# Two feed-forwards of a hybrid decoder layer: gate and up by Strassen's seven half products, down as a phase of its own

## The chip, the cores and the metric

The kernel runs on 1 core of one Trainium2 chip. The metric is the device time of one execution in microseconds (us). All outputs are float32, and every large product is made in three passes over float32r halves: each operand is split into a rounded part (`hi`) and its rest (`lo`), and hi x hi, hi x lo and lo x hi are added up.

## The reference, cut to what matters

One layer for 1088 tokens (1024 of a prompt, 64 samples), of width 1024. The change touches the feed-forward at its start and the one at its end; the attention and state-space parts between them stay.

```python
D_MODEL = 1024
D_FF = 2816
def rmsnorm(x, g):
    xf = x.astype(jnp.float32)
    xf = xf * lax.rsqrt(jnp.mean(xf * xf, axis=-1, keepdims=True) + EPS)
    return (xf * g.astype(jnp.float32)).astype(x.dtype)

def swiglu_ffn(x, g, w_in, w_out):
    h = rmsnorm(x, g) @ w_in
    gate, up = jnp.split(h, 2, axis=-1)
    return (jax.nn.silu(gate) * up) @ w_out
...
    x = x + 0.5 * swiglu_ffn(x, lw['norm_ffn1'], lw['w_ffn1_in'], lw['w_ffn1_out'])
...
    x = x + 0.5 * swiglu_ffn(x, lw['norm_ffn2'], lw['w_ffn2_in'], lw['w_ffn2_out'])
```

## The kernel before, in words

x lies in SBUF transposed: 8 tiles of 128 features by 1092 token columns, in 3 groups of 364. `ffn_stage` runs twice, as `ffn1` and `ffn2`. D_FF is 22 tiles of 128 features; a chunk is two of them, so there are 11 chunks (a loop `Fori` over the middle ones).

**Normalization** (`FusedNorm`): ACT squares x and TensorE sums the squares (in `ffn2` the sums were made by the stage before, `summed_before`), ACT takes the root, DVE the reciprocal (L220), DVE scales (L234), ACT rounds (`h_hi`, L180), DVE makes the rest (`h_lo`, L212). **Gate and up** (`up`): for each feature tile and group, gate and then up, 8 k tiles of three matmuls each (`passes`, L307 to L309), into two pairs of PSUM banks `gu`. ACT takes Silu (L411); DVE multiplies (L518), rounds (L521) and makes the rest (L523). **Down** (`down`): for 8 output tiles x 3 groups, two feature tiles of three matmuls into one of four `dn` banks; DVE adds half of it to x (L532). It stands between the two gate-and-up halves of the next chunk. **Weights** come by DMA from SP's queue, 1 MB each (`load_up`, `load_down`), each into a single raw buffer; ACT rounds (L402, L421) and DVE makes the rest (L506, L543). GpSimd does nothing in a feed-forward. The order on each engine is written out by hand in `chunk`; semaphores join them. The last chunk (`close`) also squares the finished x tiles and sums them (L264) for the next normalization; in `ffn2` the final norm and the stores of y follow.

Of the kernel before, what the change touches and what calls it, by code (L numbers as in the profile page):

```python
# [15 lines left out]
P = 128  # L16
# [295 lines left out]
def ffn_stage(core, xT, gain, h_hi, h_lo, w_in, w_out, tag, gu_banks, dn, first_loads=None, arrivals=None,  # L312
# [3 lines left out]

    nc = core.nc
    chunks = FT // 2
    with ExitStack() as ctx:
        sb = lambda name, shape, dt=F32: ctx.enter_context(nc.sbuf_tensor(f"{tag}_{name}", shape, dt))  # L320
        up_raw = sb("up_raw", [P, 2 * KT * P])
        up_hi = sb("up_hi", [P, 2, 2, KT, P], F32R)
        up_lo = sb("up_lo", [P, 2, 2, KT, P], F32R)
        down_raw = sb("down_raw", [P, 2, D_MODEL])
        down_hi = sb("down_hi", [P, 2, D_MODEL], F32R)
        down_lo = sb("down_lo", [P, 2, D_MODEL], F32R)
        act_hi = sb("act_hi", [P, 3, TP], F32R)
        act_lo = sb("act_lo", [P, 3, TP], F32R)
        silu = sb("silu", [P, 2, TG])
        prod = sb("prod", [P, 2, TG])  # L330
        gu = gu_banks[:].rearrange("p (b u) c -> p b u c", u=2)
        up_landed, up_hi_ready, up_lo_ready = map(
            core.sem, ("up_landed", "up_hi_ready", "up_lo_ready"))
        down_landed, down_hi_ready, down_lo_ready = map(
            core.sem, ("down_landed", "down_hi_ready", "down_lo_ready"))
        gu_ready, silu_ready, prod_ready, act_hi_ready, act_ready = map(
            core.sem, ("gu_ready", "silu_ready", "prod_ready", "act_hi_ready", "act_ready"))
        dn_ready, dn_added = map(core.sem, ("dn_ready", "dn_added"))
        norm = FusedNorm(core, ctx, xT, gain, ((0, KT, core.mean_model),), h_hi, h_lo, f"{tag}_norm",
                         lambda u: dn[:, u, :], (silu, prod), arrivals, gain_landed, summed_before)  # L340
        running = RunningSquares(core, lambda g: gu_banks[:, g, :], core.mean_model,
                                 [silu[:, 0, :], silu[:, 1, :], prod[:, 0, :], prod[:, 1, :]])
        lag = 3
        closing = [(t, g) for g in range(GROUPS) for t in range(KT)]
        closed = (chunks - 1) * KT * GROUPS
        fin = None
        if final is not None:
            fin = FinalNorm(core, xT, final[0], running, norm.rms[:, 0, :], norm.inv[:, 0, :], final[1])

        def slot(par, f):  # L350
            return 2 if f else par

        def schedule(eng, chunk, last):

            chunk(0, 0, True, False)
            chunk(1, 1, True, True)
            chunk(2, 0, True, True)
            with eng.Fori(1, (chunks - 3) // 2) as it:
                chunk(it * 2 + 1, 1, True, True)
                chunk(it * 2 + 2, 0, True, True)  # L360
            chunk(chunks - 2, (chunks - 2) % 2, True, True)
            chunk(chunks - 1, (chunks - 1) % 2, False, True)
            last()

        with nc.Block() as block:

            @block.sync
            def _(sp):
                def load_up(n, guard):
                    if guard:  # L370
                        sp.wait_ge(up_lo_ready, n)
                    sp.dma_start(up_raw[:], w_in[bass.ds(n, 1)].rearrange("o p c -> (o p) c")
                                 ).then_inc(up_landed, 16)

                def load_down(c, guard):
                    if guard:
                        sp.wait_ge(down_lo_ready, c)
                    sp.dma_start(down_raw[:], w_out[bass.ds(c, 1)].rearrange("o p f c -> (o p) f c")
                                 ).then_inc(down_landed, 16)

                def chunk(c, par, more, full):
                    load_down(c, full)
                    if more:
                        load_up(c * 2 + 2, True)
                        load_up(c * 2 + 3, True)

                if first_loads is not None:
                    first_loads(sp, lambda: load_up(0, False))
                else:
                    load_up(0, False)  # L390
                load_up(1, True)
                schedule(sp, chunk, lambda: None)
                if fin is not None:
                    fin.stores(sp)

            @block.scalar
            def _(act):
                def split_up(n, s, reused):
                    act.wait_ge(up_landed, n * 16 + 16)
                    if reused:  # L400
                        act.wait_ge(gu_ready, (n - 1) * GROUPS)
                    act.activation(up_hi[:, s].rearrange("p u k c -> p (u k c)"), up_raw[:],  # L402
                                   ACT.Copy).then_inc(up_hi_ready, 1)

                def gate(c, f):
                    for g in range(GROUPS):
                        j = c * 6 + (3 * f + g)
                        act.wait_ge(gu_ready, j + 1)
                        if not (isinstance(c, int) and j < 2):
                            act.wait_ge(prod_ready, j - 1)  # L410
                        act.activation(silu[:, (f + g) % 2, :], gu[:, (f + g) % 2, 0, :TG],  # L411
                                       ACT.Silu).then_inc(silu_ready, 1)

                def chunk(c, par, more, full):
                    gate(c, 0)
                    if more:
                        split_up(c * 2 + 2, 0, True)
                    act.wait_ge(down_landed, c * 16 + 16)
                    if full:
                        act.wait_ge(dn_ready, c * (KT * GROUPS))  # L420
                    act.activation(down_hi[:].rearrange("p f c -> p (f c)"),  # L421
                                   down_raw[:].rearrange("p f c -> p (f c)"), ACT.Copy
                                   ).then_inc(down_hi_ready, 1)
                    gate(c, 1)
                    if more:
                        split_up(c * 2 + 3, 1, True)

                def close():
                    for d, (t, g) in enumerate(closing):
                        act.wait_ge(dn_added, closed + d + 1)  # L430
                        running.square(act, d, xT[:, t, groups(g)])
                        if fin is not None and d in (KT + lag, 2 * KT + lag):
                            fin.roots(act, d // KT - 1)
# [7 lines left out]
            def _(pe):  # L441
# [30 lines left out]
                def chunk(c, par, more, full):  # L472
                    up(c, 0)
                    if full:
                        down(c - 1, 1 - par)
# [2337 lines left out]
```

## Time and profile before

| | |
|---|---|
| median of 3 runs (lowest to highest) | 3367.68 us (3367.06 to 3369.18) |
| the profiled execution: its span, all of its own time that the profile gives | 3370.7 us |
| TensorE busy, mean granted clock | 3002.3 us (89%), 0.913 |
| DVE, ACT, GpSimd busy | 1334.3 us (40%), 742.0 us (22%), 26.9 us (1%) |
| first feed-forward, gate and up or down from / last matmul ends | 44.6 us / 876.6 us |
| second feed-forward, first load issued / first matmul | 2500.7 us / 2511.5 us |

In the profile PE is TensorE's matmul and PEld its weight load, DVE is VectorE, ACT ScalarE, POOL GpSimd, SP SyncE, which here only issues transfers. Matmuls are pipelined: the duration of one is longer than the distance to the next, so distances between starts are what count. "PEclk" is the granted clock of TensorE as a share of 2.4 GHz. A line with "<-" says which tile is written from which.

### The profile page before, as it was taken

The page shows a single profiled execution, that of the slowest core. Times are in us where ns is not written, and L with a number is a line of the kernel's source. Part 1 is how long each engine was busy: PE and PEld are TensorE (multiplying, and loading weights), DVE is VectorE, ACT ScalarE, POOL GpSimd, SP SyncE. Part 2 cuts the span into 40 slices and gives each one's busy share as a digit, 9 for nine tenths or more (in the row PEclk, how much of TensorE's full clock was granted, in tenths as well). Part 3 has the DMA queues.
Part 4 walks back from the last instruction along what each step waited for, and adds up shares of the span by engine and source line. Part 5 has one row for each costly group of instructions (what it writes and reads, how often), then busy time and mean ns, then how long its engine had stood idle before and what let it go on. Part 6 is the DMA issues. An engine that isn't in the chain of part 4 may idle for free. (4 is left out here: it accounts for less than half of the span.)

```text
span 3370.7 us, 45917 instructions
## 1 busy us (share of the span) xinstructions
PE 3002.3 (89%) x18968; PEld 2854.1 (85%) x18968; DVE 1334.3 (40%) x2522; ACT 742.0 (22%) x1526; POOL 26.9 (1%) x43
## 2 busy tenths in 40 slices
PE   6999999999899949994999995695578999999998
PEld 5999999999699938984999992494468999999997
DVE  5333343333550031433445552624444443333434
ACT  4111100111341121211344441412332011111102
POOL 0000000000000000000000000000000000000000
PEclk8999999999899966987579996898689999999999
DMA  3111111110252330204100005002011111111101
GB/s 122 48 40 48 39 50 39 51 38 1 84 67 40 139 140 1 78 29 112 50 14 8 1 1 155 26 26 79 32 63 49 39 38 51 39 51 38 45 19 54
DMA packets 67123, 172.18 MB, mean 51 GB/s; under 512 B 11012, under 2 KB 48932, under 8 KB 56996
## 3 DMA queue, kind: packets, MB, share of 16 engines
q1 hardware_dynamic: 61940, 158.86, 15.2%
q10 hardware_dynamic: 4976, 10.31, 0.8%
q8 instruction: 160, 2.62, 0.3%
q14 instruction: 47, 0.39, 0.0%
HBM read 148.36 MB, written 24.85 MB: 51 GB/s over the span
## 5 line engine op out<-in xcount | busy, mean ns | idle before, releaser
L307 PE MATMUL ffn_down<-ffn_act_hi,ffn_down_hi 128*128 128x364 f32 x1056 | 360.9, 342 | 25.0 <-DVE x L532 20.8
L307 PE MATMUL ffn_gate_up<-h_hi,ffn_up_hi 128*128 128x364 f32 x1056 | 351.8, 333 | 23.7 <-DVE h_lo L212 13.2
L518 DVE TENSOR_TENSOR ffn_prod<-ffn_silu,ffn_gate_up 128x364 f32<-128x364 f32 x132 | 70.4, 533 | 738.8 <-ACT ffn_silu L411 738.8
L307 PE MATMUL ffn_gate_up<-h_ffn_hi,ffn_up_hi 128*128 128x364 f32 x1056 | 347.9, 329 | 6.5 <-DVE ffn_prod L518 5.4
L309 PE MATMUL ffn_gate_up<-h_hi,ffn_up_lo 128*128 128x364 f32 x1056 | 349.3, 331 | 0.9 <-issue 0.9
L308 PE MATMUL ffn_gate_up<-h_lo,ffn_up_hi 128*128 128x364 f32 x1056 | 349.9, 331 | 0.0
L309 PE MATMUL ffn_down<-ffn_act_hi,ffn_down_lo 128*128 128x364 f32 x1056 | 348.7, 330 | 0.0
L308 PE MATMUL ffn_down<-ffn_act_lo,ffn_down_hi 128*128 128x364 f32 x1056 | 348.5, 330 | 0.0
L308 PE MATMUL ffn_gate_up<-h_ffn_lo,ffn_up_hi 128*128 128x364 f32 x1056 | 347.9, 329 | 0.0
L309 PE MATMUL ffn_gate_up<-h_ffn_hi,ffn_up_lo 128*128 128x364 f32 x1056 | 347.5, 329 | 0.0
L532 DVE SCALAR_TENSOR_TENSOR x<-ffn_down,x 128x364 f32<-128x364 f32 x480 | 252.4, 536 | 178.4 <-PE ffn_down L309 177.8
L411 ACT ACTIVATE ffn_silu<-ffn_gate_up 128x364 f32<-128x364 f32 x132 | 62.5, 475 | 902.8 <-PE ffn_gate_up L309 902.8
L307 PEld LDWEIGHTS ffn_down<-ffn_act_hi,ffn_down_hi 128*128 128x128 f32 x1056 | 199.8, 189 | 35.7 <-DVE x L532 26.2
L307 PEld LDWEIGHTS ffn_gate_up<-h_hi,ffn_up_hi 128*128 128x128 f32 x1056 | 200.2, 190 | 30.7 <-issue 15.4
L307 PEld LDWEIGHTS ffn_gate_up<-h_ffn_hi,ffn_up_hi 128*128 128x128 f32 x1056 | 199.0, 188 | 7.5 <-DVE ffn_prod L518 6.1
L308 PEld LDWEIGHTS ffn_down<-ffn_act_lo,ffn_down_hi 128*128 128x128 f32 x1056 | 199.5, 189 | 4.7
L308 PEld LDWEIGHTS ffn_gate_up<-h_lo,ffn_up_hi 128*128 128x128 f32 x1056 | 200.7, 190 | 0.0
L309 PEld LDWEIGHTS ffn_gate_up<-h_hi,ffn_up_lo 128*128 128x128 f32 x1056 | 200.5, 190 | 0.0
L309 PEld LDWEIGHTS ffn_down<-ffn_act_hi,ffn_down_lo 128*128 128x128 f32 x1056 | 199.3, 189 | 0.0
L308 PEld LDWEIGHTS ffn_gate_up<-h_ffn_lo,ffn_up_hi 128*128 128x128 f32 x1056 | 199.0, 188 | 0.1
L309 PEld LDWEIGHTS ffn_gate_up<-h_ffn_hi,ffn_up_lo 128*128 128x128 f32 x1056 | 198.9, 188 | 0.0
L965 PE MATMUL ssd_hid_ps<-ssd_pages,ssd_cmp_w 128*128 128x128 f32 (+1 forms) x1280 | 171.2, 298 | 0.0
(409 smaller groups left out, 5294.0 us busy)
## 6 DMA issues: line engine op xcount, KB each, us to landing
ffn_up_raw<-in_w_ffn_in SPq DMA_DIRECT2D x44, 1024.0 KB, 4.8
ffn_down_raw<-in_w_ffn_out SPq DMA_DIRECT2D x22, 1024.0 KB, 4.9
mix_w_raw<-in_w_mix SPq DMA_DIRECT2D x20, 512.0 KB, 3.5
ssd_pages<-in_cmp_pages SPq DMA_DIRECT2D x64, 128.0 KB, 2.1
sn_slc_pages<-in_slc_pages SPq DMA_DIRECT2D x64, 128.0 KB, 2.1
x<-in_x SPq DMA_DIRECT2D x3, 1456.0 KB, 11.6
scratch_x<-x SPq DMA_DIRECT2D x1, 4368.0 KB, 13.9
out_proj<-mix_stage ACTq DMA_DIRECT2D x8, 546.0 KB, 2.8
```

Source lines behind the costliest of these rows:

```text
L307: pe.matmul(out, w_hi, x_hi, start=start, stop=False)
L308: pe.matmul(out, w_hi, x_lo, start=False, stop=False)
L309: return pe.matmul(out, w_lo, x_hi, start=False, stop=stop)
L411: act.activation(silu[:, (f + g) % 2, :], gu[:, (f + g) % 2, 0, :TG], ACT.Silu).then_inc(silu_ready, 1)
L518: dve.tensor_tensor(prod[:, b, :], silu[:, b, :], gu[:, b, 1, :TG], ALU.mult).then_inc(prod_ready, 1)
L532: dve.scalar_tensor_tensor(xT[:, t, groups(g)], dn[:, (t * GROUPS + g) % 4, :TG], 0.5, xT[:, t, groups(g)], ALU.mult, ALU.add).then_inc(dn ...
L965: mm = pe.matmul(hp[j % 2][:, 1 - later:1 - later + w].rearrange("p (b n) -> p b n", n=PAGES), w1s[:, kv, k, hh * P:(hh + 1) * P], pages[: ...
```

## The change

`ffn_stage` is rewritten; the rest of the kernel only hands it x in other pieces and frees `h_hi` and `h_lo` before the second call (with one more `clear_sems`, a barrier of all engines).

**Gate and up as a 2 x 2 block product.** A (weights) has the blocks gate and up by the first and second half of the 1024 input features; B (x times gain, not yet divided by the root mean square) has the two halves of the features by two halves of the tokens, 544 columns each, worked on in parts of 272. Seven products M1 to M7 of sums of blocks (the `PRODUCTS` table; Winograd's variant) take the place of eight. The sums of B (`T1` to `T4`, beside three of its four blocks) are made once by GpSimd in `turn`, for every k pair and part; the sums of A (`S1` to `S4`) are made by GpSimd in `combine` for every one of 22 weight tiles, in place in the single raw buffer, so in a fixed order with ACT's rounding and DVE's rest of the blocks that they overwrite. All seven A operands have one buffer of 512 columns each.

**A unit** is one weight tile by one part: 44 units of 7 products, each 4 k tiles x 3 passes of 272 columns. M6 and M7 are accumulated onto M1, M3 onto M5, M4 onto the rest, in PSUM, after ACT has copied the intermediate value out (`m1_copied`, `v_copied`, `m5_copied`) and DVE has made its addition (c11, c12, c22). M3 and M4 of a unit stand after M1 and M2 of the next one. DVE multiplies the gate by 1 / rms before and, after Silu on ACT, again; the product with up is stored to a DRAM scratch tensor. Units 0 and 1 are made k pair by k pair with seven banks, as the operands get ready.

**Down is a second phase**: 22 feature tiles in chunks of 2, 5, 5, 5 and 5; each chunk adds to x once. Activations (1088 columns) come back from DRAM and are split again (ACT rounds, DVE makes the rest), as are the weights, into the room that the operands of the first phase leave.

```diff
-        up_raw = sb("up_raw", [P, 2 * KT * P])
-        gu = gu_banks[:].rearrange("p (b u) c -> p b u c", u=2)
+HALVES, PARTS_OF_HALF, COLS = 2, 2, 272
+PRODUCTS = {"M1": (A11, B11), "M2": (A12, B21), "M3": (S4, B22), "M4": (A22, T4), "M5": (S1, T1), "M6": (S2, T2),
+            "M7": (S3, T3)}
+WIDTHS = (TG, TG, HALVES * HALF - 2 * TG)
+DOWN_CHUNKS = (2, 5, 5, 5, 5)
...
+    order = [(u, m) for u in range(2) for m in PRODUCTS]
+    for u in range(2, U):
+        late = [(u - 1, "M3"), (u - 1, "M4")] if u > 2 else []
+        order += [(u, "M1"), (u, "M2")] + late + [(u, "M6"), (u, "M5"), (u, "M7")]
+    order += [(U - 1, "M3"), (U - 1, "M4")]
...
+                def load_up(f):
+                    if f:
+                        sp.wait_ge(w_ready, N * f)
+                    sp.dma_start(raw[:].rearrange("p b c -> p (b c)"), w_in[f]).then_inc(up_landed, 16)
...
+                def turn(j):
...
+                    pool.wait_ge(scaled_x, j + 1)
+                    pool.tensor_tensor(at_(T1), extra, at_(B11), ALU.subtract).then_inc(turned, 1)
+                    pool.tensor_tensor(at_(T3), at_(B22), extra, ALU.subtract).then_inc(turned, 1)
+                    pool.wait_ge(turned, 4 * j + 1)
+                    pool.tensor_tensor(at_(T2), at_(B22), at_(T1), ALU.subtract).then_inc(turned, 1)
+                    pool.wait_ge(turned, 4 * j + 3)
+                    pool.tensor_tensor(at_(T4), at_(B21), at_(T2), ALU.subtract).then_inc(turned, 1)
...
+                    pool.wait_ge(w_ready, N * f + 1)
+                    pool.tensor_tensor(raw[:, 0], raw[:, 0], raw[:, 2], ALU.subtract).then_inc(s_made, 1)
+                    pool.wait_ge(s_made, done + 1)
+                    pool.tensor_tensor(raw[:, 2], raw[:, 2], raw[:, 3], ALU.add).then_inc(s_made, 1)
+                    pool.wait_ge(w_ready, N * f + 2)
+                    pool.tensor_tensor(raw[:, 1], raw[:, 1], raw[:, 3], ALU.subtract).then_inc(s_made, 1)
+                    pool.wait_ge(s_made, done + 3)
+                    pool.tensor_tensor(raw[:, 1], raw[:, 1], raw[:, 0], ALU.add).then_inc(s_made, 1)
...
+                    pool.tensor_tensor(w_raw[:, S2, 1, :], raw[:, 3], raw[:, 0], ALU.subtract).then_inc(s_made, 1)
...
+                for u in range(2, U):
...
+                    act.activation(gate_view(u)[:, 0, :], p_bank[:, 0:COLS], ACT.Copy).then_inc(m1_copied, 1)
                     if more:
+                        round_w(f + 1, A11)
+                        round_w(f + 1, A12)
+                    if u % 2 == 0:
+                        round_w(f, S4)
+                    gate(u - 1)
+                    if u % 2 == 0:
+                        round_w(f, A22)
+                    act.wait_ge(m_ready, made_at[u, "M6"])
...
+                    act.activation(v[:], p_bank[:, 0:COLS], ACT.Copy).then_inc(v_copied, 1)
                     if more:
+                        round_w(f + 1, S2)
+                    act.wait_ge(m_ready, made_at[u, "M5"])
+                    act.wait_ge(prod_ready, 2 * u)
+                    act.activation(u22[:], r_bank[:, 0:COLS], ACT.Copy).then_inc(m5_copied, 1)
+                    if more:
+                        round_w(f + 1, S1)
+                        round_w(f + 1, S3)
...
+                    elif m == "M7":
+                        pe.wait_ge(v_copied, u - 1)
+                        steps(p_bank, u, m, every, False, True, True).then_inc(m_ready, 1)
+                    elif m == "M3":
+                        pe.wait_ge(m5_copied, u - 1)
+                        steps(r_bank, u, m, every, False, True, True).then_inc(m_ready, 1)
+                    else:
+                        pe.wait_ge(c22_done, u - 1)
+                        steps(p_bank, u, m, every, False, True, True).then_inc(m_ready, 1)
...
+                scale(0)
+                scale(1)
+                for a in (A11, A12):
+                    rest_w(0, a)
+                rest_h(0)
+                for a in (S2, S1, S3, S4, A22):
+                    rest_w(0, a)
+                for j in range(1, PREPS):
+                    if j + 1 < PREPS:
+                        scale(j + 1)
+                    rest_h(j)
+                    if j == K_PAIRS:
+                        first_unit(0)
+                invert(0)
...
+                for u in range(2, U):
...
                     if more:
+                        rest_w(f + 1, A11)
...
+                    dve.tensor_tensor(gate_view(u)[:, 0, :], gate_view(u)[:, 0, :], unit_banks(u)[1][:, 0:COLS], ALU.add
+                                      ).then_inc(c11_done, 1)
                     if more:
+                        rest_w(f + 1, A12)
+                    if u > 2:
+                        c12(u - 1)
+                        scale_gate(u - 1)
+                    if u % 2 == 0:
+                        rest_w(f, S4)
+                    scale_twice(u - 1)
+                    multiply(u - 1)
+                    if u % 2 == 0:
+                        rest_w(f, A22)
+                    if more:
+                        rest_w(f + 1, S2)
+                        rest_w(f + 1, S1)
...
+                    dve.tensor_tensor(u22[:], u22[:], unit_banks(u)[0][:, 0:COLS], ALU.add).then_inc(c22_done, 1)
+                    if more:
+                        rest_w(f + 1, S3)
```

## Rows read from the trace of the kernel before

**Rows 1.** The page: the span, and the busy time of each engine.

```profile
span 3370.7 us, 45917 instructions
PE 3002.3 (89%) x18968; PEld 2854.1 (85%) x18968; DVE 1334.3 (40%) x2522; ACT 742.0 (22%) x1526; POOL 26.9 (1%) x43
```

**Rows 2.** Stretches: length, busy PE, PEld, DVE, ACT, POOL (us), PEclk, DMA, GB/s.

```profile
0.00:44.60 44.60, 23.37 (x49) 11.37 (x49) 18.80 (x26) 23.10 (x40) 0.20 (x4) 0.81 0.56 202
...
122.80:837.60 714.80, 700.14 (x4186) 696.54 (x4186) 272.09 (x443) 79.22 (x86) 0.00 (x0) 1.00 0.11 39
...
2511.50:2545.00 33.50, 22.79 (x97) 18.22 (x97) 30.99 (x50) 15.99 (x28) 0.00 (x0) 0.81 0.23 91
2545.00:3316.00 771.00, 757.69 (x4512) 753.80 (x4512) 288.00 (x465) 87.00 (x94) 0.00 (x0) 1.00 0.11 40
```

**Rows 3.** Timeline of PE, 364 columns, the first and last of 32.

```profile
164.67 0.33 PE L309 MATMUL ffn_gate_up<-h_ffn_hi,ffn_up_lo 128*128 128x364 f32 x1
...
169.84 0.32 PE L307 MATMUL ffn_gate_up<-h_ffn_hi,ffn_up_hi 128*128 128x364 f32 x1
```

**Rows 4.** Timeline of PE, 256 columns, the first and last of 16.

```profile
1220.06 0.28 PE L307 MATMUL mkv_ps<-h_mix_hi,mkv_w_hi 128*128 128x256 f32 x1
...
1221.82 0.28 PE L307 MATMUL mkv_ps<-h_mix_hi,mkv_w_hi 128*128 128x256 f32 x1
```

**Rows 5.** Costliest groups of DVE, shapes apart.

```profile
L518 DVE TENSOR_TENSOR ffn_prod<-ffn_silu,ffn_gate_up 128x364 f32<-128x364 f32 x132 | 70.4, 533 | 738.8 <-ACT ffn_silu L411 738.8
L521 DVE CAST ffn_act_hi<-ffn_prod 128x364 fp32r<-128x364 f32 x132 | 46.2, 350 | 4.6
...
L1510 DVE TENSOR_TENSOR mix_w_lo<-mix_w_raw,mix_w_hi 128x1024 fp32r<-128x1024 f32 x20 | 24.4, 1222 | 176.6 <-ACT mix_w_hi L1444 176.6
...
L220 DVE RECIPROCAL ffn_norm_inv_rms<-ffn_norm_rms 128x364 f32<-128x364 f32 x6 | 14.6, 2427 | 19.5 <-ACT ffn_norm_rms L172 19.5
```

**Rows 6.** Costliest groups of ACT, shapes apart.

```profile
L402 ACT ACTIVATE ffn_up_hi<-ffn_up_raw 128x2048 fp32r<-128x2048 f32 x44 | 84.0, 1909 | 2.9 <-DMA ffn_up_raw<-in_w_ffn_in 2.9
...
L1444 ACT ACTIVATE mix_w_hi<-mix_w_raw 128x1024 fp32r<-128x1024 f32 x20 | 21.1, 1057 | 7.3 <-ACT mix_stage L1484 5.7 <-DMA mix_w_raw<-in_w_mix 1.6
```

**Rows 7.** The page's DMA issues: KB each, median us to landing.

```profile
ffn_up_raw<-in_w_ffn_in SPq DMA_DIRECT2D x44, 1024.0 KB, 4.8
```

**Rows 8.** Groups of GpSimd, shapes apart.

```profile
L1132 POOL TENSOR_TENSOR ssd_c_scaled<-ssd_exp_acs,x 128x512 f32<-128x512 f32 x16 | 20.0, 1270 | 559.6 <-ACT ssd_exp_acs L1082 559.6
L1132 POOL TENSOR_TENSOR ssd_c_scaled<-ssd_exp_acs,x 128x256 f32<-128x256 f32 x2 | 1.4, 726 | 22.6 <-ACT ssd_exp_acs L1082 22.6
```

**Rows 9.** Timeline of DVE and GpSimd, alone and beside each other.

```profile
1258.36 0.69 DVE L1188 TENSOR_TENSOR ssd_x_scaled<-ssd_x_nat,ssd_to_end 128x512 f32<-128x512 f32 x1
...
1381.65 2.16 DVE L1181 TENSOR_SCALAR ssd_seg<-ssd_bc_ps,ssd_acs 128x128 f32<-128x128 f32 x8 [0.43 <-ACT ssd_exp_acs L1082]
1381.70 2.50 POOL L1132 TENSOR_TENSOR ssd_c_scaled<-ssd_exp_acs,x 128x512 f32<-128x512 f32 x2 [23.60 <-ACT ssd_exp_acs L1082]
1383.73 1.01 DVE L1188 TENSOR_TENSOR ssd_x_scaled<-ssd_x_nat,ssd_to_end 128x512 f32<-128x512 f32 x1
```

**Rows 10.** The chain of waits around the closing chunk of the second.

```profile
3316.03 2.13 issue
...
3319.54 0.30 PE ffn_down L307
...
3323.94 0.61 PE ffn_gate_up L264 x2
```

**Rows 11.** Timeline at a clear_sems: DVE's last, SP's next.

```profile
2454.83 0.23 DVE L2476 TENSOR_TENSOR h_lo<-ma_o_ps,h_hi 128x64 fp32r<-128x64 f32 x1 [3.19 <-ACT h_hi L2445]
...
2456.19 0.80 SPq L608 DMA_DIRECT2D memout_w_raw<-in_w_mem_out  x2
```

**Rows 12.** Timeline: the first feed-forward's last matmuls, the second's first load.

```profile
875.23 1.39 PE L264 MATMUL ffn_gate_up<-ffn_prod,const_mean_model 128*128 128x364 f32 x4
...
2500.74 9.35 SPq L372 DMA_DIRECT2D ffn_up_raw<-in_w_ffn_in  x2
```

More of the change, by code:

```diff
@@ L343, in ffn_stage @@
         lag = 3
-        closing = [(t, g) for g in range(GROUPS) for t in range(KT)]
-        closed = (chunks - 1) * KT * GROUPS
         fin = None
         if final is not None:
[L348 to L363, printed above, removed]
+            fin = FinalNorm(core, xT, final[0], running, fin_rows[:, 0, :], fin_rows[:, 1, :], final[1])
@@ new lines, in landing, with par, unit_banks, gate_view @@
+        def landing(sems, i):
+            c = chunk_of[i]
+            n = i - first_k[c]
+            if c == 0:
+                return sems[5 + n], 16
+            before = sum(1 for e in range(c) if e % 2 == c % 2 and n < DOWN_CHUNKS[e])
+            return sems[(0 if c % 2 else 5) + n], 16 * (before + 1)
+        def par(u):
+            return u % 2
+        def unit_banks(u):
+            return (bank(0), bank(1), bank(2)) if par(u) == 0 else (bank(3), bank(4), bank(5))
+        def gate_view(u):
+            return sums[:, par(u)]
@@ L396, in _, with fresh @@
+            def fresh(a):
+                return {A11: raw[:, 0], A12: raw[:, 1], S2: w_raw[:, S2, 1, :], S1: raw[:, 2], S3: raw[:, 0],
+                        S4: raw[:, 1], A22: raw[:, 3]}[a]
             @block.scalar
             def _(act):
[L398 to L403, printed above, removed]
@@ L428, in close @@
[L428 to L433, printed above, removed]
-                    if fin is not None:
-                        fin.roots(act, GROUPS - 1)
-                norm.scalar(act, [lambda: split_up(0, 0, False), lambda: split_up(1, 1, False)])
@@ new lines, in invert, with c12 @@
+                def invert(g):
+                    if summed_before:
+                        dve.wait_ge(rms_ready, GROUPS)
+                    else:
+                        dve.wait_ge(rms_ready, (g + 1) * HALVES)
+                    part = inv_view(g)
+                    dve.reciprocal(part, part).then_inc(inv_ready, 1)
+                    dve.wait_ge(inv_ready, g + 1)
+                def c12(u):
+                    dve.wait_ge(m_ready, made_at[u, "M3"])
+                    dve.wait_ge(v_copied, u - 1)
+                    dve.tensor_tensor(gate_view(u)[:, 1, :], v[:], unit_banks(u)[2][:, 0:COLS], ALU.add
+                                      ).then_inc(c12_done, 1)
```

634 lines of the change are left out of this document (457 added, 177 removed).

## The prediction

> **What bounds it now.** The page first [rows 1]: TensorE is busy for 89% of the span, with DVE at 40% and GpSimd at 1%. The table by stretches says where that is so [rows 2]: in both feed-forwards, TensorE's clock is granted in full (1.00, the 2.4 GHz level) and 4512 matmuls take 771 us, 0.171 us each. Only their first part differs: 44.6 us before the first matmul of the first one, and in 2511.5 to 2545 DVE is busy 31.0 of 33.5 us while TensorE waits for prepared rows. So fewer matmul columns are worth their time, if the other engines deliver. Next, the spacing of back-to-back matmuls: 31 of 364 columns in 5.17 us, 0.1668 us each [rows 3]; 15 of 256 columns in 1.76 us, 0.1173 us each [rows 4]. The page's 330 ns for one is latency. Then the price list: DVE [rows 5], ACT [rows 6], transfers [rows 7], GpSimd [rows 8], and how DVE and GpSimd run beside each other [rows 9].
>
> **The columns removed.** Gate and up now take 44 units x 7 products x 4 k tiles x 3 passes = 3696 matmuls of 272 columns where 3168 of 364 stood. A straight line through the two spacings gives 0.1246 us for 272 columns: 3696 x 0.1246 = 460.5 us against 3168 x 0.1668 = 528.4 us. One product (12 matmuls) is 1.50 us, a unit 10.47 us, one weight tile (two units) 20.93 us. Down keeps 1584 matmuls, a third of them of 360 columns: 263.5 us. If everything else were hidden, each feed-forward would gain 68 us, and the stalls of today's chunks (0.171 against 0.167, 20 us) besides. The rest of this text is what is not hidden.
>
> **Prices of the new work.** From [rows 5], by a straight line, DVE takes about 0.44 us for 272 columns, 0.69 for 512, 0.72 for 544, 1.29 for 1088, 2.14 for 1904. From [rows 6], ACT takes 0.4 us for 272, 0.63 for 512, 0.65 for 544, 1.79 for 1904. GpSimd takes 1.27 us for 512 and 0.72 for 256, so 0.76 for 272 [rows 8]. Per weight tile that is DVE 7 x 0.69 + 2 x 3.6 = 12.0 us, ACT 8.2, GpSimd 5 x 1.27 = 6.4, all under 20.93. By shares nothing becomes the bound; by order of dependence something may.
>
> **DVE beside GpSimd.** The one place where they overlap [rows 9]: the same 512-column product of two SBUF tensors takes 0.69 us with GpSimd idle and 1.01 us when it starts 0.47 us before GpSimd ends (1381.70 + 2.50 = 1384.20); it ends 0.54 us after that, so it looks blocked until GpSimd is through, with its fixed part hidden. The eight operations with one PSUM input ahead of it ran 0.27 us apart under GpSimd. I take it as exclusive in both directions for two-SBUF-input DVE operations; the other direction (GpSimd held by DVE) no row shows, and its bounds are 0 and the length of the DVE operation. The Trainium skill (SBUF — State Buffer, "Who interferes with whom") says so too: whichever starts first holds the shared ports for its whole instruction, and a tensor_tensor with both inputs in SBUF competes with GpSimd's reads; the row agrees for DVE's side. By it the sum is the one below, without it the first rival's.
>
> **The steady loop.** The raw weight tile has one buffer, so this ring closes once per tile. Time 0 is the end of DVE's `u22` addition (c22) of an odd unit. DVE then: S3 rest, c11, c12, scale_gate, S4 rest, scale_twice, two products, A22 rest; done at 4.9. SP issues load_up, behind the act store; 4.8 us to land [rows 7] and 0.3 for the store before it: 10.0. ACT rounds A11 (10.6), DVE takes its rest (11.35). GpSimd now makes five sums. Unblocked, with 0.05 us of wait each: 18.0. Exclusive, four DVE operations come between them (A12 rest, scale_gate, scale_twice, second product); each adds what is left after its hidden part, about 0.5, 0.55, 0.5 and 0.3, and some of GpSimd's fixed part is hidden in return: 19.15. ACT, which stands waiting for S2 in its queue, rounds it (19.8), and only then copies M5 into `u22` (20.2), which M3 waits for; then it rounds S1, DVE takes the rest of S1 and does c22: 21.9. ACT's copy of `v` stands behind the gate's Silu there too, so M7 starts at 16.05, a microsecond late. With waits between dependent GpSimd operations of up to 0.1 us I take **22.3 us per tile** against TensorE's 20.93; bounds 20.93 (not blocked: the ring is 20.8) and 24.4 (see the third rival). TensorE then stands 1.4 us in 22.3. Before the closing chunk it stood 2.13 us, and soon after it ran 0.30 us a matmul, the lower level (1.2 GHz), until about 3322.5 [rows 10]. Should 1.4 us do the same, 3 us at half speed cost 1.5 us, which is no more than it has to wait anyway: I add nothing.
>
> **The start of each.** x is no longer normalized first, so DVE can begin at once, but eight rounds (four k pairs x two column blocks) must each pass scale (three operations, 0.9 us if DVE copies at the two-column rate of its cast, 350 ns for 364 columns [rows 5], else 1.6), GpSimd's four differences (3.1 us), ACT's rounding (1.8) and DVE's rest (2.14). Exclusive, one round costs 0.9 + 3.1 + 2.14 = 6.1 us on the shared path; with the first tile's weights (6.4 + 7 x 0.65) and about 3 us of DVE idle while it stands at S2, the last `h` is ready at 8 x 6.15 + 11 + 3 = 63 us. Behind it in a row: the last 21 matmuls (2.8), invert (544 columns of reciprocal at 6.67 ns, 3.6), scale, Silu, scale, products (3.0), the act store (2.2) which first_unit(1) waits for since `prod` is reused, its seven additions (3.0), A11 rest, the five sums of tile 1 that wait for it (7.4), S2, S1, S3, a second invert, and the unit's tail until load_up(2). That load goes out at 91.3, where in the steady loop it comes 10.2 after the unit's M1: unit 2 starts in effect at **82 us** in the second feed-forward, **88** in the first (x and weights must land, table loads, squares). Unblocked: 64.5 and 70.5.
>
> **Between the phases.** The last gate passes c12, scale, Silu, scale, products (2.2 us after TensorE's last M4), then DVE splits two activations and two weight rows of chunk 0: 7.0 us during which TensorE stands, since `k_ready` needs all four. I add 2.5 us for a clock at the lower level after it, an estimate: after 2.13 us of standing some 3 us ran at half speed [rows 10] and 2 us because chunk 0 gives DVE 24 additions and 10 splits in 24 us. Chunks 1 to 4 have 59 us each for the same DVE work, and 5 MB of loads: hidden. Running sums as before: 24 x 0.61 [rows 10]. The extra clear_sems with its barrier: 1.1 us at most, the gap there between DVE's last end and the first issue [rows 11].
>
> **The sum.** Second feed-forward: 1.1 + 82 + 20 x 22.3 + 20.9 + 7 + 2.5 + 2 + 263.5 + 14.6 = 839.6 us; before it ran from 2500.74 [rows 12] to about 3357 (the closing chunk starts at 3318.2 after the wait [rows 10] and takes 24 x 1.61), 856.4: gain 16.8. First: 88 in place of 82, no clear: 844.5, against 875.23 + 1.39 = 876.6 [rows 12]: gain 32.1. Together 48.9. The profiled execution gives only its span, 3370.7, 3.0 above the median of the runs, 3367.68; what lies around it is not seen and unchanged. 3367.7 - 48.9 = **3319 us**.
>
> **Rivals.**
> 1. *DVE and GpSimd do not hold each other up* (only the one row speaks for blocking). The ring is 20.8, TensorE bounds at 20.93, starts are 17.5 us shorter: 2 x (17.5 + 20 x 1.37) = 90 more, **3229**. Chance 0.20. Half of it (blocking on DVE's side alone, about 3275): 0.10.
> 2. *Forecast*, 3290 to 3350: 0.46.
> 3. *GpSimd becomes the bound* (slower). Place: the five sums between A11's rest and S2, ahead of ACT's copy of M5. If one costs 1.7 us instead of 1.27 (dependent operations, each waiting for its predecessor, or losing more than one turn to DVE's queue), the ring is 24.4 and the change ends at 3319 + 40 x 2.1 = **3403**. It decides from 0.25 us more per sum (48.9 / 200) on. For it: the rows of GpSimd are only of independent pairs under a DVE that reads PSUM. Against: 1268 ns is steady to 1%. Chance 0.24, of which 0.06 within 0.2%.
>
> **Range and chances.** 80%: 3229 to 3385, from the unblocked ring to a ring of about 23.9; the forecast's own is 3290 to 3350. Under 3361 (0.2%, about what a measurement of this kernel tells from no change) 0.76, within 0.06, above 0.18.
>
> **What would show it.** Matmul spacing of 0.125 us in a product; a period of 22.3 us between load_up issues; S2's rounding on ACT waiting for GpSimd; DVE's 512-column operations longer than 0.69 us on average (1.0) and GpSimd's longer than 1.27 if it is held too; TensorE's waits before M3 and M4 ending with ACT's `u22` copy or DVE's c22; the first M1 of unit 2 near 82 us into the second feed-forward, some 7 us of standing before chunk 0. Wrong if the 272-column spacing is not on the line, if the period is 20.9 or over 23.5, or if the granted clock falls in the steady part.

## The result, and the profile after

The changed kernel takes 3406.14 us (3401.44 to 3407.55), the kernel before, on the same chip, 3368.43 us: a ratio of 1.0112, 95% interval 1.0098 to 1.0127. The forecast was 3319 us with 3229 to 3385 as its range; the change made the kernel 37.7 us slower. The page of the changed kernel, span and engines [rows 1]:

```profile
span 3405.5 us, 49715 instructions
PE 2919.5 (86%) x20104; PEld 2774.3 (81%) x20104; DVE 1555.5 (46%) x2766; ACT 972.5 (29%) x2021; POOL 426.4 (13%) x328
```

TensorE did lose 83 us of busy time, and the span still grew by 34.8: what was taken out of it came back as standing. The table by stretches of the changed kernel says where (columns as in [rows 2]):

```profile
33.00:107.00 74.00, 40.02 (x223) 38.79 (x222) 20.35 (x28) 19.38 (x17) 14.85 (x20) 0.75 0.00 1
144.20:582.80 438.60, 409.86 (x3182) 402.61 (x3182) 260.54 (x399) 139.18 (x284) 146.61 (x95) 1.00 0.21 71
621.90:629.00 7.10, 0.31 (x2) 0.29 (x2) 6.19 (x7) 5.39 (x6) 0.00 (x0) 0.79 1.02 416
2538.90:2627.40 88.50, 41.98 (x227) 39.83 (x228) 58.73 (x71) 28.73 (x34) 51.10 (x42) 0.73 0.08 27
2627.40:3065.50 438.10, 411.28 (x3183) 404.05 (x3182) 260.25 (x400) 139.18 (x284) 146.56 (x95) 1.00 0.21 71
```

The first row is the start of the first feed-forward, with its clock at 0.75; the second and fifth are 19 periods of the loop each, 23.08 and 23.06 us a weight tile; the third is the standing ahead of chunk 0; the fourth is the whole start of the second feed-forward. The issues of the up loads on SP's timeline, from the third tile's (the first number is the start) to the last; 17 are left out:

```profile
144.22 1.21 SPq L491 DMA_DIRECT2D ffn_w_raw<-in_w_ffn_in  x1
167.41 0.56 SPq L491 DMA_DIRECT2D ffn_w_raw<-in_w_ffn_in  x1
...
582.84 0.56 SPq L491 DMA_DIRECT2D ffn_w_raw<-in_w_ffn_in  x1
```

The spacing of 272 columns, TensorE's timeline, first and last of 36 [rows 3, 4]:

```profile
617.22 0.29 PE L712 MATMUL ffn_gate_up<-ffn_h_hi,ffn_w 128*128 128x272 f32 x1
...
621.63 0.29 PE L714 MATMUL ffn_gate_up<-ffn_h_hi,ffn_w 128*128 128x272 f32 x1
```

4.41 us over 35 intervals is 0.126 us (forecast 0.1246), so TensorE alone needs 168 x 0.126 = 21.17 us a tile, and the loop stands 1.9 us in every 23.07. The groups of the operations that share the weight tile, shapes apart [rows 5, 8]:

```profile
L837 DVE TENSOR_TENSOR ffn_w<-ffn_w_raw,ffn_w 128x512 fp32r<-128x512 f32 x264 | 224.1, 852 | 170.5 <-ACT ffn_w L603 165.9
L573 POOL TENSOR_TENSOR ffn_w_raw<-ffn_w_raw 128x512 f32<-128x512 f32 x44 | 75.2, 1710 | 0.0
L882 DVE TENSOR_TENSOR ffn_prod<-ffn_sums,ffn_u 128x272 f32<-128x272 f32 x88 | 63.3, 719 | 0.0
L881 DVE TENSOR_TENSOR ffn_prod<-ffn_sums,ffn_gate_up 128x272 f32<-128x272 f32 x84 | 36.8, 438 | 2.9
```

DVE's 512-column rest takes 852 ns on the mean and GpSimd's third sum 1710, where each alone takes 690 and 1270 [rows 8, 9]. The second product (L882), with both inputs in SBUF, takes 719 ns; the first (L881), with one input in PSUM, 438, although the two stand side by side. Each engine holds the other up. GpSimd's timeline shows the direction of which no row of before spoke: a 272-column difference of 0.77 us becomes 2.66 us while DVE's 1904-column rest runs.

```profile
2572.11 0.77 POOL L558 TENSOR_TENSOR ffn_h_raw<-ffn_h_raw,ffn_b 128x272 f32<-128x272 f32 x1
2572.84 2.66 POOL L560 TENSOR_TENSOR ffn_h_raw<-ffn_h_raw 128x272 f32<-128x272 f32 x1
```

**The chain of waits** through one period of the loop (start, length, what; of TensorE's 36 single matmuls between 2849.36 and 2854.16 the first is shown):

```profile
2835.64 5.32 DMA ffn_w_raw<-in_w_ffn_in
...
2840.98 0.64 ACT ffn_w L603
...
2842.68 1.64 DVE ffn_w L837
2844.32 0.36 DVE ffn_sums L896
...
2844.77 1.29 DVE ffn_sums L866
...
2846.09 0.67 ACT ffn_sums L626
...
2846.78 1.00 DVE ffn_sums L870
...
2847.80 0.44 DVE ffn_prod L881
2848.24 0.99 DVE ffn_prod L882
...
2849.36 0.37 PE ffn_gate_up L712
...
2854.18 0.45 DVE ffn_sums L896
...
2854.72 0.74 DVE ffn_sums L866
...
2856.17 0.74 DVE ffn_sums L870
...
2857.37 0.35 DVE ffn_prod L882
2857.72 0.61 DVE ffn_w L837
...
2858.36 5.29 DMA ffn_w_raw<-in_w_ffn_in
```

This is a closed ring, and not the one forecast. It runs from the load over DVE's rest of A12, the gate's two scales and the two products to the M1 that waits for them (its bank is the one that the first product reads), then M1, M2 and M3 on TensorE, the next gate, the rest of A22 and the next load. GpSimd's five sums do not stand in it. They make it long: four DVE operations in it take 1.64, 1.29, 1.00 and 0.99 us where the same ones later in the period, with GpSimd idle, take 0.61, 0.74, 0.74 and 0.35. That is 2.48 us. TensorE's waits from 2700 to 2900 us agree:

```profile
PE ffn_gate_up L712 <- ACT ffn_v L676: 6.9, 9, 1.3
PE ffn_gate_up L712 <- DVE ffn_prod L882: 4.1, 9, 0.5
```

It waits for the copy of `v`, which stands behind the gate's Silu, and for the second product. It never waits for `u22` or c22, which were to end the wait by the forecast. M1's wait counts both products, though the second reads `u22` and not M1's bank; a wait for the first alone was not tried, and by an estimate from the 4.1 us in 9 waits could give at most 0.5 us a tile.

**The start of the first feed-forward.** ACT's timeline in the changed kernel, and TensorE's for the same round:

```profile
44.86 1.11 ACT L609 ACTIVATE ffn_h_squares<-x 128x1088 f32<-128x1088 f32 x1 [8.95 <-PE ffn_gate_up L725]
45.88 1.77 ACT L615 ACTIVATE ffn_h_hi<-ffn_h_raw 128x1904 fp32r<-128x1904 f32 x1
57.51 1.11 ACT L609 ACTIVATE ffn_h_squares<-x 128x1088 f32<-128x1088 f32 x1 [9.85 <-PE ffn_gate_up L725]
```

```profile
49.88 0.59 PE L712 MATMUL ffn_gate_up<-ffn_h_hi,ffn_w 128*128 128x272 f32 x1 [5.12 <-DVE ffn_h_lo L832]
```

A second ring: ACT's squares of a k pair have one buffer, so they wait for TensorE's sums of the pair before (L725), which stand in its queue behind that pair's 21 products, which wait for the rest of h, which waits for ACT's rounding behind the squares. A round takes some 12 us, TensorE stands 5.12 us in it, and its clock is low behind that: 37 matmuls took 6.66 us at a mean granted clock of 0.68 right behind one such wait (0.227 us from one 272-column matmul to the next at first, the 1.2 GHz level, then 0.126). The load of the third tile leaves at 144.2 us, where the forecast's steps give 97.3 (its 91.3 and the 6 us between 82 and 88). In the second feed-forward, which squares nothing here, it leaves 88.5 us after the first load (forecast 91.3).

### The profile page after: what moved, and what is told of

It reads as the page before. It is cut to its first block and busy times, and to the rows that moved or that the text cites. A ratio compares the mean times of both kernels' runs of the same rounds, so it can differ in the third digit from the quotient of the medians.

```text
span 3405.5 us, 49715 instructions
## 1 busy us (share of the span) xinstructions
PE 2919.5 (86%) x20104; PEld 2774.3 (81%) x20104; DVE 1555.5 (46%) x2766; ACT 972.5 (29%) x2021; POOL 426.4 (13%) x328
## 5 line engine op out<-in xcount | busy, mean ns | idle before, releaser
L712 PE MATMUL ffn_gate_up<-ffn_h_hi,ffn_w 128*128 128x272 f32 x1912 | 573.5, 300 | 183.2 <-DVE ffn_h_lo L832 66.5
L714 PE MATMUL ffn_gate_up<-ffn_h_hi,ffn_w 128*128 128x272 f32 x1912 | 563.8, 295 | 0.0
L713 PE MATMUL ffn_gate_up<-ffn_h_lo,ffn_w 128*128 128x272 f32 x1912 | 562.4, 294 | 0.0
L712 PEld LDWEIGHTS ffn_gate_up<-ffn_h_hi,ffn_w 128*128 128x128 f32 x1912 | 370.8, 194 | 203.7 <-issue 92.3
L713 PEld LDWEIGHTS ffn_gate_up<-ffn_h_lo,ffn_w 128*128 128x128 f32 x1912 | 371.7, 194 | 0.0
L714 PEld LDWEIGHTS ffn_gate_up<-ffn_h_hi,ffn_w 128*128 128x128 f32 x1912 | 371.1, 194 | 0.0
L837 DVE TENSOR_TENSOR ffn_w<-ffn_w_raw,ffn_w 128x512 fp32r<-128x512 f32 x264 | 224.1, 852 | 170.5 <-ACT ffn_w L603 165.9
L307 PE MATMUL mix_ps<-h_mix_hi,mix_w_hi 128*128 128x364 f32 x480 | 161.6, 337 | 9.0 <-issue 6.0
L1390 PEld LDWEIGHTS ssd_hid_ps<-ssd_pages,ssd_cmp_w 128*128 128x128 f32 x1280 | 163.8, 211 | 2.6
L712 PE MATMUL ffn_down<-ffn_h_hi,ffn_w 128*128 128x272 f32 x552 | 163.0, 295 | 0.0
L714 PE MATMUL ffn_down<-ffn_h_hi,ffn_w 128*128 128x272 f32 x552 | 162.5, 294 | 0.0
L713 PE MATMUL ffn_down<-ffn_h_lo,ffn_w 128*128 128x272 f32 x552 | 162.3, 294 | 0.0
L308 PE MATMUL mix_ps<-h_mix_lo,mix_w_hi 128*128 128x364 f32 x480 | 160.3, 334 | 0.0
```

What stands on the lines that cost most here:

```text
L307: pe.matmul(out, w_hi, x_hi, start=start, stop=False)
L308: pe.matmul(out, w_hi, x_lo, start=False, stop=False)
L712: pe.matmul(out, hi, x_hi, start=start, stop=False, skip_group_check=chained)
L713: pe.matmul(out, hi, x_lo, start=False, stop=False, skip_group_check=chained)
L714: mm = pe.matmul(out, lo, x_hi, start=False, stop=stop, skip_group_check=chained)
L837: dve.tensor_tensor(w[:, a, 1, :], fresh(a), w[:, a, 0, :].bitcast(F32), ALU.subtract).then_inc(w_ready, 1)
```

## The experiments

All times are medians; each ratio is to runs of the kernel before on the same chip at the same time. "Third load" is the issue of the up load that ends the start, from time 0 in the first feed-forward and from the first load in the second (of its second half, where the load goes in halves); "period" is the mean of 19. Third load and period are those of one profiled execution each.

| run | us | ratio to before, 95% | third load | period |
|---|---|---|---|---|
| changed kernel | 3406.1 | 1.0112 (1.0098 to 1.0127) | 144.2, 88.5 | 23.08, 23.06 |
| squares earlier | 3365.1 | 1.0000 (0.9986 to 1.0014) | 110.9, 88.3 | 23.04, 22.96 |
| load in halves | 3323.1 | 0.9877 (0.9856 to 0.9898) | 145.0, 87.9 | 21.20, 21.11 |
| start reordered | 3389.9 | 1.0070 (1.0053 to 1.0086) | 140.6, 84.4 | 22.88, 22.89 |
| all three | 3284.6 | 0.9752 (0.9736 to 0.9769) | 109.8, 84.0 | 21.25, 21.16 |
| one column | 3312.6 | 0.9837 (0.9809 to 0.9865) | 140.5, 83.1 | 21.23, 21.16 |
| settings | 3325.0 | 0.9874 (0.9845 to 0.9902) | 142.9, 87.3 | 21.18, 21.18 |
| load ahead of the store | 3391.7 | 1.0071 (1.0047 to 1.0094) | 145.0, 88.5 | 22.91, 22.87 |
| second feed-forward alone | 3362.9 | 0.9990 (0.9975 to 1.0006) | -, 88.4 | -, 22.89 |
| all three, h rounded first | 3272.6 | 0.9720 (0.9694 to 0.9746) | 105.1, 84.0 | 21.17, 21.16 |
| and chunk 0 ready earlier | 3265.3 | 0.9704 (0.9682 to 0.9726) | 103.6, 84.1 | 21.24, 21.16 |
| settings, short | 3327.0 | 0.9878 (0.9831 to 0.9925) | 143.3, 88.4 | 21.23, 21.32 |
| settings, long | 3378.5 | 1.0024 (1.0002 to 1.0046) | 146.2, 89.5 | 22.35, 22.46 |

### Squares earlier: the ring of the start

```diff
                         pe.wait_ge(h_ready, u * K_PAIRS + kp + 1)
...
+                        elif not summed_before and kp:
+                            square_sums(u * K_PAIRS + kp)
...
-                        if not summed_before and u * K_PAIRS + kp < PREPS - 1:
+                        if not summed_before and kp == 0:
```

The added lines stand ahead of that wait; `root(0)` on ACT then waits for unit 0's M7 as well.

> First feed-forward only: TensorE sums the squares of k pair j before the 21 products of pair j-1's successor, as soon as ACT has squared them, and no longer behind the products of the pair before. Theory 'start ring through TensorE' (one squares buffer: square, sum, products, next square; 11.7 us a round in the changed kernel's trace, 33 to 107 us): the rounds fall to the 6 to 7 us that DVE and GpSimd alone need (the second feed-forward's rounds), the second tile's load leaves 25 to 35 us earlier than at 144.2 us, and the whole is 25 to 35 us shorter than the changed kernel. Rival 'the shared work of DVE and GpSimd, or the arrival of x, sets the start': the load leaves within 5 us of 144.2 and the time stays within 5 us. The steady period stays at 23.1 us by both.

The load left 33.3 us earlier and the kernel was level with the one before. The ring is shown to be the cause, at some 33 us in the profile and 37.7 by the ratios, a little more than expected. Behind a standing of 1.74 us, a stretch of 6.7 us now held 54 matmuls at full clock, where the one above, behind 5.12 us, held 37.

```profile
36.80:43.50 6.70, 6.67 (x54) 6.67 (x55) 6.06 (x7) 2.93 (x3) 5.23 (x5) 1.00 0.01 2
```

### Load in halves, and load ahead of the store: the ring of the raw tile

```diff
+                def load_half(f, b):
                     if f:
-                        sp.wait_ge(w_ready, N * f)
+                        sp.wait_ge(w_ready, N * f - 2 * (1 - b))
...
+                    if more:
+                        load_half(u // 2 + 1, 0)
+                    store(u - 1)
+                    if more:
+                        load_half(u // 2 + 1, 1)
```

> The load of the next up tile is split into two transfers: quarters 0 and 2 of the tile go as soon as DVE has the rest of S3 (two DVE rests before the end of the tile), ahead of the act store, quarters 1 and 3 at the old place. Theory 'the ring of the one raw weight tile sets the period, 23.07 us': A11's rounding and S3's sum start about 2 us or more earlier, the ring falls under what TensorE needs (7 x 1.51 x 2 = 21.2 us), the load's period becomes 21.2 to 21.8 us, and 38 periods give 50 to 72 us: 3335 to 3357 against 3406. Rival 'the sum of DVE's and GpSimd's work under the lock sets the period': it stays at 22.8 to 23.1 us and the time within 10 us.

```diff
+                store(0)
                 for u in range(2, U - 1):
-                    store(u - 2 if u == 2 else u - 1)
-                    if u == 2:
-                        store(1)
                     if u % 2 == 0 and u // 2 + 1 < FT:
                         load_up(u // 2 + 1)
+                    store(u - 1)
```

> Only the order of two issues on SP: the up tile's load goes out ahead of the act store and no longer behind it. Theory 'the landing is in the ring, 5.5 us behind the store against the 4.8 of one alone': the landing is 0.5 to 0.7 us shorter and the period falls by as much, to 22.4 to 22.6 us, 20 to 25 us in all. Rival 'the two transfers share the queues whichever is issued first': no change of the landing, time within 5 us.

Halves: 19 periods in 402.7 us, TensorE busy for 401.7 of them, though DVE's 512-column operations still take 795 ns and GpSimd's third sum 1761. The time fell further than expected. The edit does three things at once: half of the load leaves two DVE operations earlier, it leaves ahead of the store, and A11's rounding waits for that half alone (4.1 us to land, the median). So it is the ring's length, not either engine's amount of work, that costs the 1.9 us a tile.

```profile
145.00:547.70 402.70, 401.68 (x3182) 401.13 (x3181) 256.44 (x399) 141.07 (x284) 147.00 (x95) 1.00 0.23 77
```

The order of the two issues alone missed its expectation: the periods are 0.18 us shorter, not 0.5 to 0.7. Even that is not shown to be the order's. The loop as the changed kernel has it ran at 22.88 to 23.08 us a period in the four kernels that keep it, and the median landing, 5.6 us in the changed kernel, is 5.4 both here and with the squares earlier, where the store still goes first. The time fell by 14 us, which the rival ("within 5 us") does not cover either. In the profiled executions, 16.0 us apart, 6.9 us lie in the periods and 6.9 in the stretch between the feed-forwards, which the edit does not touch. Where the gain comes from stays open.

### One column and settings: what GpSimd does to the ring

The four kernels here leave out the sums of A from the second tile on. With one column, ACT and DVE also take S2 straight from the raw block. A setting is GpSimd's `memset` to zero, which writes SBUF and reads nothing.

```diff
+                    n = 1 if f else K_PAIRS * P
-                    pool.tensor_tensor(raw[:, 0], raw[:, 0], raw[:, 2], ALU.subtract).then_inc(s_made, 1)
+                    pool.tensor_tensor(raw[:, 0, 0:n], raw[:, 0, 0:n], raw[:, 2, 0:n], ALU.subtract).then_inc(s_made, 1)
```

> GpSimd's five sums of each up tile cover one column instead of 512 from the second tile on, so S2, S1, S3 and S4 are not the sums of A: their arithmetic is left out, everything else is kept. Theory 'GpSimd's chain of 7.9 us is in the ring of the raw weight tile': the ring loses some 6 us or more, TensorE becomes the bound, the period between loads falls from 23.07 to 21.2 us, and DVE's 512-column operations return to 0.69 us. Rival 'transfer, ACT and DVE set the period alone': it stays above 22.5 us.

```diff
+                        pool.memset(out, 0.0).then_inc(half_set, 1)
+                        pool.wait_ge(half_set, next(steps))
+                        pool.memset(out, 0.0).then_inc(s_made, 1)
```

> Each of GpSimd's five sums from the second tile on is replaced by two settings to zero of 512 columns with a wait between them, about as long in all, which read nothing from SBUF: the sums of A are left out. Theory 'GpSimd's reads of SBUF and DVE's two-input operations exclude each other': DVE's 512-column operations return to 0.69 us from 0.85, the chain on GpSimd has no turn to wait and takes 5 times its own two settings, and the period falls to some 21.5 us. Rival 'the chain is long by its own steps and waits': the period stays near 23 us.

The short settings add a third one of 64 columns to each sum, the long ones one of 352.

> As the experiment with settings to zero (from the second tile on the five sums of A are left out), but with three settings a sum, 512, 512 and 64 columns, so that a sum takes about the 1.27 us of a GpSimd sum that nobody holds up: a chain of 6.5 to 6.7 us against 7.9 in the changed kernel and 5.6 in the first such experiment, with no reads of SBUF. Theory 'the 1.3 us by which DVE's turns lengthen the chain are what lifts the ring over TensorE's 21.2 us': 14.2 us of the ring outside the chain plus 6.6 is 20.8, so the period stays at TensorE's 21.2 us. Rival 'the first such experiment gained only because its chain was shorter than any real one': over 22 us.

> The same with 512, 512 and 352 columns, about 1.6 us a sum (the sums of A are left out here too): a chain as long as in the changed kernel, 7.9 to 8.2 us, but with DVE never held up. Theory 'the length of GpSimd's chain sets the period': 14.2 to 15.0 plus 8.0, 22.2 to 23.0 us, though DVE's 512-column operations take 0.69 us. Rival 'DVE's lengthened operations set it': 21.2 us.

With one column, the period is TensorE's, 21.2 us, and DVE's rests take 694 ns: GpSimd's sums are in the ring or hold up what is in it. With settings to zero in place of sums, DVE's 512-column rests take 695 or 696 ns on the mean at all three lengths of the chain (groups of the one with two settings, shapes apart):

```profile
L848 DVE TENSOR_TENSOR ffn_w<-ffn_w_raw,ffn_w 128x512 fp32r<-128x512 f32 x264 | 182.5, 695 | 164.4 <-ACT ffn_w L614 159.9
```

So what holds DVE up is GpSimd's sums, which read SBUF, and not that GpSimd is busy. The Trainium skill (SBUF — State Buffer, "Who interferes with whom") calls the port pair that the two share an exclusive lock and the only cause of contention; by it a DVE instruction with two SBUF inputs contends with a GpSimd one that reads SBUF, not with one that only writes. The 852 and 695 ns agree, and so do the 2.66 us of GpSimd above. The chains measure 5.6, 6.6 and 7.8 us. The first two leave TensorE as the bound. The third is as long as the real chain (7.9) and gives 22.4 us, against the real kernel's 23.07. And TensorE waits for something else in it, from 2700 to 2900 us (its L725 is the products' matmul, L712 of the changed kernel; L694 is the copy of M5 into `u22`):

```profile
PE ffn_down L725 <- ACT ffn_u L694: 7.3, 9, 1.0
PE ffn_gate_up L725 <- ACT ffn_v L689: 0.7, 2, 0.4
```

There are two rings of nearly one length. The one of the forecast, through GpSimd's chain, S2 and the `u22` copy, is 22.4 us at a chain of 7.8: this one is shown by the three lengths. The one through DVE's held-up operations is 23.07 and covers it: this is read from the chain and the waits of the changed kernel and from the 0.7 us that are left, for no run holds DVE up beside a short chain on GpSimd. With GpSimd neither reading nor slow, both fall under 21.2.

### Start reordered, and one feed-forward alone

```diff
+                for a in (A11, A12):
+                    rest_w(1, a)
                 invert(0)
...
+                invert(1)
                 first_unit(1)
-                for a in (A11, A12, S2, S1, S3):
+                for a in (S2, S1, S3):
                     rest_w(1, a)
-                invert(1)
```

ACT's rounds of A11 and A12 move in the same way.

> The work of the first two units in another order: ACT's rounds and DVE's rests of A11 and A12 of tile 1 come ahead of unit 0's gate, and unit 1's reciprocal ahead of the seven sums of its first half product. Theory 'the start is a row of dependent steps': the five sums of tile 1 on GpSimd, which waited for A11's rest, run beside the gate, and the second tile's load leaves 8 to 10 us earlier in each feed-forward: 15 to 20 us in all. Rival 'the order moves only the wait': within 3 us. The steady period stays at 23.1 us by both.

The load left 3.6 and 4.1 us earlier, against 8 to 10 expected. The periods were 0.2 us shorter, 7 us over both, though the loop had not changed; with the second feed-forward alone, where it had not changed either, they are 22.89 us too, so this is scatter between executions. The time fell by 14 us, of which the starts are 7.7 in the profile.

> The change in the second feed-forward alone; the first keeps the stage, layouts and square sums of the kernel before. Theory: of the loss of 35 us by the profiled executions, 32 lie in the first feed-forward and -2 in the second, the rest between: so 3365 to 3375 us, within 0.2% of the kernel before, and the first feed-forward takes its 877 us again. Rival 'half the loss comes from each': 3385 to 3390.

3362.9 us, level with the kernel before: the second feed-forward, as changed, neither gains nor loses, and the loss is the first one's.

### All three, and two steps further

> The three edits of the other kernels of this call together: squares summed ahead of the products, the up tile's load in two halves, the second tile's first rounds ahead of the gate. If the three losses lie behind one another in time and do not share a cause, the gains add: 28 + 60 + 18, so 3290 to 3315 us, 50 to 80 us under the kernel before. If the period is set by work and not by the ring, only the starts are gained: 3355 to 3365.

The gains nearly add: 37.7, 79 and 14 us by the ratios are 131, and the three together give 121, somewhat more than expected.

```diff
                 for j in range(1, PREPS):
-                    if not summed_before:
+                    last = j == PREPS - 1
+                    if not summed_before and last:
                         square(j)
-                        if j == PREPS - 1:
-                            root(1)
+                        root(1)
                     round_h(j)
...
+                    if not summed_before and not last:
+                        square(j)
```

> The kernel of all three edits, and in its first feed-forward ACT rounds k pair j's h before it squares pair j, not behind it (but for the last pair, whose place holds the squares). In the trace of the first experiment the squares of pairs 1 and 4 still stood 7.7 and 9.6 us for TensorE's sums, and h's rounding behind them. Theory 'what is left of the first start is that queue order': the second tile's load leaves 8 to 14 us earlier, 3271 to 3277 us against 3285. Rival 'TensorE would have stood for the weights and for unit 0's seven sums anyway': within 3 us.

The time fell by 12.1 us by the medians, as expected, and by 10.8 by the ratios, whose intervals just overlap. But the load left only 4.7 us earlier, where at least 8 were expected. Another 5.8 us of the profiled executions' difference lie between the last up load of the first feed-forward and the first of the second, where the two kernels are the same. In the executions that leave that stretch as it is, it takes from 1944 to 1956 us, so a comparison of two single executions carries scatter of 5 us and, at worst, 12; 4.7 us are all that the reordering is shown to give.

```diff
+                    if u == U - 1:
+                        split_act(0)
                     dve.wait_ge(m5_copied, u - 1)
...
+                split_act(1)
                 c12(U - 1)
                 scale_gate(U - 1)
+                split_down(0)
+                split_down(1)
                 scale_twice(U - 1)
                 multiply(U - 1)
-                for i in range(first_k[1]):
-                    split_act(i)
-                    split_down(i)
```

> The kernel of the line above, and chunk 0 of down is made ready ahead of the last gate: ACT rounds its two activations and two weight rows right behind the last unit's copies, DVE splits them around c22 and the last scale, and the last Silu's scaling and products come behind. Theory 'TensorE stands 7 us between the phases because DVE does the last gate and four splits in a row': the standing falls to 2.5 to 3.5 us in each feed-forward, 8 to 10 us in all against the kernel of the line above. Rival 'the loads of chunk 0 or the clock take what is gained': under 3 us.

TensorE's timeline at chunk 0's first matmul in the first feed-forward, first without this edit and then with it:

```profile
550.75 0.67 PE L307 MATMUL ffn_down<-ffn_h_hi,ffn_wd_a 128*128 128x364 f32 x1 [6.79 <-DVE ffn_w L981]
```

```profile
546.12 0.43 PE L307 MATMUL ffn_down<-ffn_h_hi,ffn_wd_a 128*128 128x364 f32 x1 [2.23 <-DVE ffn_w L936]
```

The standing falls from 6.79 to 2.23 us in both feed-forwards, 9.1 us, a little further than expected; the medians differ by 7.3, a little less than expected, and the intervals of the two ratios overlap. The granted clock in the 5 us behind it was 0.57 without the edit and 0.65 with it, so a shorter wait gives little of the clock back. This kernel, 3265.3 us, is 3.0% faster than the one before the change.

## Why the prediction was wrong, point by point

The prediction's terms against the changed kernel's execution (its miss there is 3405.5 - 3321.8 = 83.7 us):

| step | forecast | measured | off by |
|---|---|---|---|
| start of the first, to the third load | 97.3 | 144.2 | +46.9 |
| start of the second | 91.3 | 88.5 | -2.8 |
| 19 periods, first | 423.7 | 438.6 | +14.9 |
| 19 periods, second | 423.7 | 438.1 | +14.4 |
| last up load to the end of the sums, both | 2 x 323.5 | 326.1 + 328.2 | +7.3 |
| between the feed-forwards, clear included | 1625.2 | 1630.0 | +4.8 |
| behind the second's sums | 13.6 | 11.8 | -1.8 |

- **The columns removed: right.** 0.126 us for 272 columns against 0.1246, and a loop bound by TensorE, once the ring is shorter, takes 21.2 us against 20.93.
- **DVE beside GpSimd: right, both directions.** The first rival (no blocking, 3229 us) is out. The settings, whose DVE is never held, came to 3325 us.
- **The steady loop: a ring priced rightly that is not the longest.** Its ring was followed through GpSimd's sums, S2, the `u22` copy and c22, with DVE's held-up time charged to GpSimd's chain. That chain came out as forecast (7.8 us from A11's rest to S2, 7.9 measured), and the ring through it is 22.4 against the forecast's 22.3. What was not followed is the same held-up time on DVE's side: 2.48 us on the A12 rest, both scales and the second product, behind which M1 waits. The forecast had the wait for `v` (M7 "a microsecond late"; it is 6.9 us in 9 waits), but not that this path closes a ring of its own, 23.07 us. The step that failed is "and only then copies M5 into `u22` (20.2), which M3 waits for": that is not the wait that ends last. A landing of 5.6 us (the median) in place of 5.1 adds to both rings. That the period came within 0.8 us of the forecast is luck in so far as the two rings are nearly equal; over 38 periods it still cost 29.3 us.
- **The start of each: right for the second, and the failed step for the first**: "88 in the first (x and weights must land, table loads, squares)". Squares were charged as some ACT time. They are a wait, through TensorE's queue and one buffer, and it cost 33 of the 46.9 us, as the first experiment shows. The rest of that row was not taken apart fully: in that experiment's trace ACT's squares of pairs 1 and 4 still waited 7.7 and 9.6 us for TensorE, and rounding h first took back 4.7 us; some 9 us stay open.
- **Between the phases: right in the main.** 6.79 us of standing against 7.0, and chunk 0 at a low clock. The 2.6 and 4.7 us by which the parts from the last up load to the end of the sums are longer were not taken apart.
- **The third rival** (slower, since a GpSimd sum costs 1.7 us instead of 1.27) came nearest in time, 3403 us, and its mark is there: the third sum takes 1.71 us. But the mean of the five is 1.56, and its ring of 24.4 us did not come: 23.07. Most of the loss was the start's.
- **A term for scatter was missing.** A stretch that no edit touches differed by up to 12 us between executions.

## What to carry to other kernels

Where an operand has one buffer, follow every engine's path from its release back to itself, not only the longest-looking one: here two rings lay 0.7 us apart, and a step that first reads as "held up for half a microsecond" stood four times in the second. A helper computation with one buffer that passes through TensorE's queue (squares, then their sums) must be queued ahead of the products that its successor feeds, or it turns the whole start into a chain. When removed work on the bound engine gives nothing back, shorten the ring before giving up the change: issuing half of the load two operations earlier, and ahead of the store, was worth 2.3% here. And before a small difference between two traces is given a cause, look at a stretch that neither edit touches: here it moved by up to 12 us.

## What the runs showed of the hardware that had not been expected

- The lock works both ways, and the loser pays the remainder of the other's operation: GpSimd's 0.77 us became 2.66 under DVE's 1904 columns, DVE's 0.61 became 1.64 under GpSimd's 512. GpSimd's settings to zero, which write SBUF and read nothing, left DVE at 695 ns, of which the prediction had said nothing.
- A 1 MB load with the 272 KB store beside it took 5.4 us to land when it was issued ahead of the store, and 5.4 or 5.6 behind it (medians of three kernels); it had been 4.8 in the kernel before [rows 7].
- Chunk 0 ran at a granted clock of 0.65 in its first 5 us even where TensorE had stood only 2.23 us.
